# A causal depthwise convolution moved from VectorE to banded products on TensorE, and key selection in three groups of tiles in place of five

## The reference, cut to what matters

```python
u, gc, q, k, v, ga, iq, ik, iw = project(rmsnorm(x), w_in)          # u = ua * sigmoid(ub), 512 channels
y  = depthwise_causal_conv(u, w[31 taps, 512]) + b                  # y[t, c] = sum_j w[j, c] * u[t - 30 + j, c]
cy = silu(layernorm_over_channels(y) * ln_g + ln_b)
score[t, s] = sum_h iw[t, h] * relu(iq[t, h] . ik[s])               # 4 indexer heads, causal
idx = top_k(score, 256)                                             # 128 for the sample tokens
o   = softmax(q . k[idx] / 8 + t5_bias) @ v[idx]                    # 8 heads, 2 key heads
x   = x + concat(cy * silu(gc), o * silu(ga)) @ w_out ; y_out = rmsnorm(x)
```

## Time and profile before

| what | us |
|---|---|
| median of 3 runs (1946.81 to 1954.7) | 1948.4 |
| the profiled execution: time | 1948.56 |
| the profiled execution: span of the trace | 1946.9 |
| mean granted clock of TensorE | 0.895 of full speed |
| busy: PE / DVE / ACT / POOL | 1531.3 / 1366.8 / 737.0 / 407.8 |

### The profile page before, as it was taken

The page is one execution under the profiler, slowest core; times in us unless marked ns, Lnnn a source line. Parts: engine busy times, 40 slices in busy tenths (PEclk is TensorE's granted clock), DMA queues, the critical chain, the costliest instruction groups (busy, mean ns, idle before and its releaser), DMA issues. The chain is left out here.

```text
span 1946.9 us, 26700 instructions
## 1 busy us (share of the span) xinstructions
PE 1531.3 (79%) x9511; PEld 1287.0 (66%) x9511; DVE 1366.8 (70%) x2361; ACT 737.0 (38%) x1271; POOL 407.8 (21%) x297
## 2 busy tenths in 40 slices
PE   6879959699659939792768888888888767369998
PEld 5876959689649939792456666665665545247776
DVE  3413988688879888886259998988789997134442
ACT  3525411332142232231214554555445444344441
POOL 2120314234204303431300100001000111232211
PEclk9989979899879969896768998999899997579999
DMA  7632452113256402321511110110102111613333
GB/s 243 211 73 47 95 95 69 66 52 91 65 199 139 101 21 74 93 59 42 159 56 47 41 54 1 54 54 29 52 28 76 37 49 61 203 65 129 120 125 108
DMA packets 166186, 164.59 MB, mean 85 GB/s; under 512 B 54666, under 2 KB 137618, under 8 KB 166047
## 3 DMA queue, kind: packets, MB, share of 16 engines
q1 hardware_dynamic: 165031, 160.80, 27.9%
q0 software_dynamic: 1024, 2.10, 0.3%
HBM read 100.94 MB, written 57.93 MB: 82 GB/s over the span
## 5 line engine op out<-in xcount | busy, mean ns | idle before, releaser
L674 PE MATMUL psum<-xh,wh 128*128 128x384 f32 (+1 forms) x1056 | 348.1, 330 | 34.0 <-POOL wl L550 32.5
L1256 DVE SCALAR_TENSOR_TENSOR cy<-cu,cw,cy 128x1088 f32<-128x1088 f32 x240 | 350.3, 1460 | 15.8 <-issue 0.7
L674 PE MATMUL psum<-xh,wl 128*128 128x384 f32 (+1 forms) x1056 | 347.1, 329 | 0.0
L674 PE MATMUL psum<-xl,wh 128*128 128x384 f32 (+1 forms) x1056 | 347.1, 329 | 0.0
L1159 ACT ACTIVATE pts<-psT 128x512 f32<-128x512 f32 (+1 forms) x302 | 168.5, 573 | 314.9 <-PE psT L1426 292.3
L674 PEld LDWEIGHTS psum<-xh,wh 128*128 128x128 f32 x1056 | 200.3, 190 | 35.8 <-issue 21.4
L1418 PE MATMUL psU<-kh,qt 128*128 128x512 f32 (+3 forms) x320 | 138.5, 434 | 92.2 <-DVE mx L1310 90.9
L1442 PE MATMUL psO<-pts,vs 128*64 128x128 f32 x2176 | 185.2, 292 | 23.6 <-ACT pts L1159 23.4
L674 PEld LDWEIGHTS psum<-xl,wh 128*128 128x128 f32 x1056 | 200.5, 190 | 0.0
L674 PEld LDWEIGHTS psum<-xh,wl 128*128 128x128 f32 x1056 | 200.2, 190 | 0.0
L1426 PE MATMUL psT<-cst,L 128*128 128x128 f32 x1105 | 184.8, 300 | 11.0 <-ACT L L1187 10.7
(11 more groups left out here) (270 smaller groups left out, 2535.1 us busy)
## 6 DMA issues: line engine op xcount, KB each, us to landing
wst<-in_w_in SPq DMA_DIRECT2D x28, 512.0 KB
wst<-in_w_in SPq DMA_DIRECT2D x32, 256.0 KB
qt<-d_q SPq DMA_DIRECT2D x16, 512.0 KB, 4.1
xst<-in_x_prompt SPq DMA_DIRECT2D x15, 512.0 KB, 3.9
xr<-in_x_prompt SPq DMA_DIRECT2D x15, 512.0 KB, 4.4
out_y_prompt<-fin SPq DMA_DIRECT2D x15, 512.0 KB, 2.9
gate<-d_ga SPq DMA_DIRECT2D x17, 256.0 KB, 4.4
d_mix<-mix SPq DMA_DIRECT2D x17, 256.0 KB, 2.1
```

What stands on the lines that cost most here:

```text
L674: last = nc.tensor.matmul(u[:, 0:k * P], a[:, w % 2, cc, :], x[:, s0:s0 + k, cc, :], start=(cc == 0 and e == 0), stop=(cc == KC - 1 and e ...
L1256: V.scalar_tensor_tensor(y, u[:, k:k + HALFW], w, y, ALU.mult, ALU.add)
```

## The change

**Selection.** Three groups of 3, 4 and 8 tiles take the place of five groups of three. Each group's scores lie one behind the other in one buffer, and the arrays of the search have as many columns as the group has tiles. The group of tiles 10 to 13 is scored at the same place as the second group was, the group of tiles 2 to 9 at chunk 7 of the second half. The two indexer jobs for tiles 0 and 1 are left out, which no score uses.

**Convolution, first part.** The projected `u` is transposed on PE (jobs `uT`, one behind the next `proj` job) and written to DRAM with tokens on partitions (`d_un`). The write of the bias rows `d_r` (1.5 MB) goes from SP's queue at chunk 4 to ACT's queue at the block's start.

**Convolution, second part.** DVE's 248 taps are gone. A window of 32 outputs of one channel is a product of a 64x32 band matrix (the taps, taken from `d_cw` with a shift of one row for each column: `ht`) with the 64 inputs around it (`uw`); 73 windows (64 of the prompt, one of its remainder, 8 of the samples) are the moving operand. For each of 4 x 32 columns there are four such products, one for each quarter of the array's columns, from partitions 0 to 63 or 64 to 127. 20 jobs of up to 28 products run at the end of steps 2 to 16, into the two `psT` buffers; DVE adds the bias and stores them (`yc`). Each quarter of the channels (`q`) is loaded by 16 DMAs, when the one before is through (`load_windows`). From step 18 on the layer norm is done here too, for two tiles every fourth step: sums on DVE, a product with `avg` on PE, subtraction on DVE, squares on POOL, sums, product, power on POOL, scaling on DVE, and products with a flip matrix that bring channels back to partitions (`turn`).

**Output block.** Stages a and b, the samples' convolution and its transposes are gone; stage c stays, and ACT's copies of the last five weight chunks stand together behind the first one.

```diff
-SCORE_AT = {(0, 2): 0, (0, 13): 1, (1, 0): 2, (1, 9): 3, (1, 17): 4}
-GROUPS = [[16, 15, 14], [13, 12, 11], [10, 9, 8], [7, 6, 5], [4, 3, 2]]
+SCORE_AT = {(0, 2): 0, (0, 13): 1, (1, 7): 2}
+GROUPS = [[16, 15, 14], [13, 12, 11, 10], [9, 8, 7, 6, 5, 4, 3, 2]]
...
+            for b in range(len(blocks)):
+
+                if not (name == "iq" and max(blocks[b]) < 2):
+                    jobs.append(("proj", h, c, b))
+                put_late()
+                if name == "ua":
+                    late.append(("uT", h, j, b))
...
-                if (h, c) == (0, 4):
-                    sp.dma_start(t.d_r.rearrange("t h x -> h t x"), mem.rrow[:, :].unsqueeze(1).to_broadcast([NH, P, BANDX])).then_inc(r_out, 16)
...
             high(0)
+            act.dma_start(t.d_r.rearrange("t h x -> h t x"), mem.rrow[:, :].unsqueeze(1).to_broadcast([NH, P, BANDX])).then_inc(r_out, 16)
...
-                        dve.wait_ge(mask_ready, 3 * gno + c)
+                        dve.wait_ge(mask_ready, selected(gno) + c)
...
+NQ, QA = 4, 32
+BANKA = 512 // NW
+CONV_JOBS = [(q, a, min(BANKA, QA - a)) for q in range(NQ) for a in range(0, QA, BANKA)]
+PER_Q = len(CONV_JOBS) // NQ
+CONV_STEPS = [(2, 3, 3, 4, 4), (6, 7, 7, 8, 8), (10, 11, 11, 12, 12), (14, 15, 15, 16, 16)]
+CONV_STEP = [x for q in CONV_STEPS for x in q]
+
+NORM = [[LAST]] + [[i - 1, i] for i in range(LAST - 1, 0, -2)]
+SUM_STEP = [18 + 4 * k for k in range(len(NORM))]
+SQ_STEP = [s + 3 for s in SUM_STEP]
+TURN_STEP = [s + 5 for s in SUM_STEP]
...
+            def load_windows(q):
+                if q:
+                    sp.wait_ge(pe_pt, last_conv(q - 1))
...
-            def conv_tap(tap):
...
-                    V.scalar_tensor_tensor(y, u[:, k:k + HALFW], w, y, ALU.mult, ALU.add)
...
+            def convolved(e, q, a, k):
+
+                c, pt = slice(q * QA + a, q * QA + a + k), PT[:, pt_no["C", e] % 2]
+                if e == 0:
+                    dve.wait_ge(cb_in, 64)
+                dve.wait_ge(pe_pt, pt_no["C", e] + 1)
+                TT(yc[:, :, c].rearrange("p n a -> p a n"), pt[:, 0:k * NW].rearrange("p (a n) -> p a n", n=NW),
+                   cbt[:, c].unsqueeze(2).to_broadcast([128, k, NW]), ALU.add).then_inc(conv_out, 1)
...
+            def convolve(e, q, a, k):
+                pt = take_pt(("C", e))
+                if a == 0:
+                    pe.wait_ge(ht_in, 32 * (q + 1))
+                    pe.wait_ge(uw_in, 224 * (q + 1))
+                for x in range(k):
+                    for g in range(4):
+                        r, c = g // 2, QA * (g % 2) + a + x
+                        last = T.matmul(pt[WIN * g:WIN * g + WIN, x * NW:(x + 1) * NW], ht[64 * r:64 * r + WROWS, :, c],
+                                        uw[64 * r:64 * r + WROWS, :, c], start=True, stop=True,
+                                        tile_position=(64 * r, WIN * g))
+                last.then_inc(pe_pt, 1)
...
-        stages = [(stage, k) for k in range(2) for stage in "abc"]
-        schedule = stages[:5] + [("tile", LAST)] + stages[5:]
+        schedule = [("c", 0), ("tile", LAST), ("c", 1)]
```

More of the change, by code:

```diff
@@ L90, in constants @@
     at("ones")[:] = 1.0 / C
+    for r in range(128):
+        at("flip")[r, r // WIN * WIN + WIN - 1 - r % WIN] = 1
+        at("avg")[r, r % WIN::WIN] = 1.0 / C
     return c
@@ L372, in select_jobs, with put_late @@
 def select_jobs():
-    jobs = []
+    jobs, late = [], []
+    def put_late():
+        jobs.extend(late)
+        late.clear()
     for h, blocks in enumerate(HALVES):
@@ L451, in project_and_select, with slot_free @@
         stage_no = {s[0]: m for m, s in enumerate(staged_jobs)}
-        dmas = lambda kind: 4 if kind in ("iq", "q") else 1
+        dmas = lambda kind: {"iq": 4, "q": 4, "ua": 0}.get(kind, 1)
+        ut_jobs = [n for n, j in enumerate(jobs) if j[0] == "uT"]
+        ut_of = {jobs[n][1:]: (q, n) for q, n in enumerate(ut_jobs)}
+        stage_of_u = {(s[3], s[2], s[4]): m for m, s in enumerate(staged_jobs) if s[1] == "ua"}
+        ut_zero, z_out = sem("ut_zero"), sem("z_out")
+        ut_out = [sem(f"ut_out{s}") for s in range(2)]
         def slot_written(eng, m):
             eng.wait_ge(out_s[m % 2], 16 * sum(dmas(s[1]) for s in staged_jobs[m % 2:m + 1:2]))
+        def slot_free(eng, m):
+            _, kind, j, h, b = staged_jobs[m]
+            if kind == "ua":
+                eng.wait_ge(pe_job, ut_of[h, j, b][1] + 1)
+            else:
+                slot_written(eng, m)
         def slots(h, b):
@@ L685, in _ @@
                         last = nc.tensor.matmul(u[:, b0:b0 + bn], q, mem.ikl[:, a + b0:a + b0 + bn], start=False, stop=True)
+                elif job[0] == "uT":
+                    m = stage_of_u[job[1:]]
+                    pe.wait_ge(combined, m + 1)
+                    for e in range(slots(job[1], job[3])[1]):
+                        last = nc.tensor.transpose(u[:, e * P:(e + 1) * P], ust[:, m % 2, e * P:(e + 1) * P], ident)
                 elif job[0] == "we":
@@ L941, in attend_and_convolve @@
     band0 = lambda i: max(0, (i - 1) * P)
-    dconv = [(c, h) for h in range(2) for c in range(CC)]
-    def spread(widths, units):
-        total, work = sum(widths[:-2]), len(units) * TAPS
-        return [min(work, -(-work * sum(widths[:n]) // total)) for n in range(len(widths) + 1)]
-    dtaps = spread([width(i) for i, _ in pairs], dconv)
     LW = NT * P
```

584 lines of the change are left out of this document (333 added, 251 removed).

## The result

| what | before | after |
|---|---|---|
| median of the runs, us | 1949.2 | 1866.8 (1866.3 to 1873.8) |
| ratio, 95% interval | | 0.958 (0.955 to 0.961) |
| profiled execution: time, span | 1948.6, 1946.9 | 1866.6, 1864.9 |
| busy PE / DVE / ACT / POOL | 1531.3 / 1366.8 / 737.0 / 407.8 | 1518.8 / 994.3 / 735.8 / 435.7 |

82 us faster, where 125 were forecast; the time lies in the stated range. The changed kernel by block, to be laid beside the earlier trace rows: selection, start of the attention, its steps, head and body of the output block.

A forecast was written before the change was run, and what follows sets the result against it. No engine fills the span: DVE bounds selection, PE and DVE trade places in attention, PE bounds the output block. Selection −53, attention −37 and output −35 sum to −125 on 1948.6, giving 1824 us; range 1778 to 1890.

The forecast's parts named there:

- which now goes out at the block's start: Selection: the 1.5 MB `d_r` write moves off SP's queue to the block's start; no cost was counted there.
- the 9.6 that I counted as won: Selection: DVE's pick at 363.21 waited for ACT, behind PE and the `d_r` write; removing that wait gains 9.6 us.
- PE has done its 44 chunks by about 838 and is no bound: Selection: PE finishes its chunks by about 838 us, ahead of the block's forecast end at 864, so does not limit it.
- the new wait: Selection: DVE's second pick of group 1 waits for ACT's mask copy behind chunk 6, from about 565 to 602: 36 us.
- 40 for a group's fixed part: Selection: each group costs 40 us that does not grow with its keys, so two groups fewer give 80.
- the window products: Attention steps: 1,024 float32 passes on PE's path at 0.044 us each add 45 us.
- the shortest step of each tile: Attention: without taps every step takes its tile's shortest time, 62 steps falling from 636.7 to 538 us: −99.
- rival D: Window products: operands strided by 256 bytes read four times slower, 0.25 us a pass, +212, total 2036; chance 0.05.
- Weights should be through at about 1708 to 1710: Output block head: ACT's last five weight copies stand together, so weights are ready sooner: −12 of the 59.6 us.
- C: Window products: a column's four products run one after another at 0.11 us, +67, total 1891; chance 0.16.
- E: Attention: window loads take 40 us per quarter, not 25; PE waits some 15 at steps 6, 10, 14: +45, 1869; chance 0.10.
- B: Selection: ACT's copies come before DVE needs them, so the 36 us wait vanishes, total 1788; chance 0.14.

The follow-up runs named there:

- experiment 5: Kernel before the change, with only the write of `d_r` moved from SP's queue at chunk 4 to ACT's queue at the block's start: 1971.4 us against 1951.5, ratio 1.010.
- experiment 2: Changed kernel with the second half's indexer chunks at 2 and 3 and the third group's scores at chunk 4 instead of 7: 1868.7 us, ratio 0.957.
- experiment 3: Changed kernel with third group's scores at chunk 4, indexer chunks at 2 and 3, and ACT's last-group mask copies between jobs of chunks 19 to 21: 1846.2 us.
- Experiment 1: Changed kernel with the write of `d_r` issued by ACT ahead of chunk 17 of the second half instead of at the block's start: 1868.7 us, ratio 0.957.
- experiment 6: Changed kernel with five groups of three tiles and their places as before the change: 1904.8 us, ratio 0.975.
- Experiment 7: Changed kernel with the output block's weights, gates and norm vectors loaded in one piece of 128 rows, channels exchanged so output wrong: 1850.9 us, ratio 0.949.

## Why the forecast was right in sign and too large by half

**"which now goes out at the block's start", priced at nothing: the step that failed in the selection.** The second group starts at 395.2 where I had 368.9, and both chains of the block, DVE's and PE's, are late by these 26.3 before it. Of them 3.7 stand ahead of the block, 15.8 are the write: it holds up SP's issues for 19 us, and I took away its stall at chunk 4 without asking what stands behind it at the new place. The last 6.7 are the first group's length, 203.1 for 196.4: the 9.6 that I counted as won were no full gain, since DVE had been faster during that stall (experiment 5). The second group adds 5.3 (259.8, with its wait of 38.3, for 218.5 + 36), the third nothing. That is 31.6 of DVE's chain, all of the missing 32.

**Selection, "PE has done its 44 chunks by about 838 and is no bound": wrong too, and hidden behind the first.** I followed DVE's chain to 864 and checked PE only by the end of its projections. But ACT's copies of the last group stand behind PE's last job, and 28 us of picks wait for them, one by one. My own numbers gave 838 + 2 + 28 = 868, 4 over my 864; with PE's true end, 866, it is 896. In the changed kernel DVE's chain comes to the same place, so this tie costs 3.4 there; it takes what is gained ahead of it. Experiments 2 and 3 show this: 28 us less of waiting brought nothing until the copies moved, and then 22. Experiment 1 shows it less cleanly, since its write stalls PE near the block's end: by the third group's start, 16.1 earlier than in the changed kernel, I would estimate PE's end at 850 without that stall, and it was 869.

**The sum of the new wait** has two slips that cancel in part: 368.9 + 29.5 + 112.6 is 511.0 and not 512.5, and 25 ahead of 587.4 is 562.5 and not 565. Put right, the wait is 37.7; it measured 38.3.

**40 for a group's fixed part** was about right: with both waits out of it the chain ran nearly as reckoned (196.4, 218.5 and 240.8 forecast; 203.1, 221.5 and 237.4 measured, the second being 259.8 less the wait of 38.3, the third 240.8, from 655.0 to 895.9, less 3.4). These are 662 us against the 742.3 of five groups (experiment 6): a gross of 80, as forecast. The two waits, 41.6, leave a net of 38; without the first of them PE's end would have taken as much (experiment 2).

**Attention: right, with two sizes off that cancel.** Start -11.8 (-10). The 62 steps fell from 636.7 to 610.7. Of that the window products are 38.3 (45) and the norm 35.6: 7.2 for the means and variances, 21.7 for the turns, 6.7 for waits of the turns (20 and some of the 7 in the forecast). What is left is 536.8, against 538 from the shortest step of each tile. That the 45 was near is luck: I took a price near that of adjacent products in halves of the array, and argued that the column step was free (rival D: "none is shown slow"). The true base is 0.0184, and the step of 256 bytes doubles it. Rival D's mechanism is real; its factor was 2, not 4, on less than a third of its base of 0.063. The rule of the Trainium skill that the forecast set against the cheap price ("TensorE: Matmul & The Clock Gate", Part 3: weight loads overlap products in flight only if their row group differs) would have given nearer 112; the trace shows 38.3, and 18.8 with adjacent operands.

**Output block: body -27.7 (-23), head +4.9 (-12).** The head failed by 17: I counted ACT's order and not the loads. "Weights should be through at about 1708 to 1710" took their arrival as given, while the change cut the gates and half of the weights into pieces of 32 partitions. Experiment 7 gives the 15.2 us back and lands at 49.3, one from my 48.

So the rivals: C (0.11 a pass, 0.0374 measured), E (a wait of 15 for loads, none measured) and B (no wait at the pick, 38.3 measured) are out; D has the right mechanism and the wrong size; the case that came was on no list. The range was said to take in C, whose 1891 lies 1 above its end.

## What to carry to other kernels

When two engines share one ordered list, ask of the end of a block what stands behind the last job of each, not only whose chain is longest: here a copy in ACT's order tied DVE's last 28 us to PE's last product, and 28 us less of waiting upstream were worth nothing until it moved. When a layout is turned so that one stage can read it, follow the turn to every load that must now arrive in pieces, and to every operand that is now read with a step; both cost a factor of two here, 15 and 19 us. A large write held up the issues behind it at each of the places where it was put, so look for the place where the waiting engines have slack, and measure it.

## What the runs showed of the hardware that was not expected

- Loads into 32 partitions: 190 GB/s with all 16 DMA engines busy; into 128: 335 to 342.
- Three DMAs by the outermost dimension of their access patterns: 2 of 16 DMA engines busy for 2 (52 GB/s), about 8 for 8 (56 GB/s), and 1 for 127 (26 GB/s). While the write of `d_r` was on its way, two issues of another queue together lasted 12 to 24 us.
- Four 64x32 float32 products of 73 adjacent columns run at 0.0184 us a pass, 0.074 for the four. One of them alone would take 0.063, an estimate from the 0.86 ns a column of 64-row weights. So products in different quarters overlap, also those of the same rows: two by two one after the other would be 0.126.
- A moving operand with a step of 256 bytes doubles that; the step of the weights costs next to nothing beside it (19.2 us against 18.8 for 1,024 passes).
- An operation on 3 elements takes DVE 0.51 us in the kernel before, 0.89 in the changed one and 0.93 in experiment 5, mean of the same eight.
